# Attention head statistics in four partition groups

## The reference, cut to what matters

```python
h = rmsnorm(x, p['mix_norm'])
z = h @ p['w_in']                       # q 12x128 | k 12x128 | v 12x128 | u | gates
q = z[..., :ATT_WIDTH].reshape(B, L, N_ATT_HEADS, HEAD_DIM)
k = z[..., ATT_WIDTH:2 * ATT_WIDTH].reshape(B, L, N_ATT_HEADS, HEAD_DIM)
q = rope(rmsnorm(q, p['q_norm']), pos)
k = rope(rmsnorm(k, p['k_norm']), pos)

def rmsnorm(x, gain):                   # here over the 128 channels of one head
    y = x * rsqrt(mean(x * x, axis=-1) + 1e-6)
    return y * gain
```

## Time and profile before

| | |
|---|---|
| three timed runs | 2300.42, 2302.45, 2301.75 us; median 2301.75 |
| the profiled execution | 2301.55 us, of which the span of the trace is 2299.8 us |
| granted TensorE clock, mean | 0.998 of full speed |
| busy in the span | PE 2272.1 us (99%), DVE 1404.6 (61%), ACT 995.0 (43%), POOL 535.9 (23%) |
| iterations x = 1 to 12 | about 880 to 1033 us of the span, clock 1.00 |

### The profile page before, as it was taken

The page is one execution under the profiler, slowest core; times in us unless marked ns, Lnnn a source line. Parts: engine busy times, 40 slices in busy tenths (PEclk is TensorE's granted clock), DMA queues, the critical chain, the costliest instruction groups (busy, mean ns, idle before and its releaser), DMA issues.

```text
span 2299.8 us, 47445 instructions
## 1 busy us (share of the span) xinstructions
PE 2272.1 (99%) x18546; PEld 2255.7 (98%) x18546; DVE 1404.6 (61%) x1414; ACT 995.0 (43%) x1219; POOL 535.9 (23%) x565
## 2 busy tenths in 40 slices
PE   7999999999999999999999999999999999999999
PEld 7999999999999999999999999999999999999998
DVE  6566457775455667886657777655554455544555
ACT  5644333333344543444445555444433344333442
POOL 3795026650000204664405540110000000000000
PEclk9999999999999999999999999999999999999999
DMA  7888777777777688758848865568787777657864
GB/s 209 265 246 284 227 242 248 256 260 246 236 238 224 202 262 260 229 180 284 300 145 307 283 197 186 174 202 270 239 243 224 241 246 250 219 184 222 246 199 139
DMA packets 435222, 535.65 MB, mean 233 GB/s; under 512 B 27744, under 2 KB 415832, under 8 KB 431272
## 3 DMA queue, kind: packets, MB, share of 16 engines
q1 hardware_dynamic: 420224, 511.58, 70.7%
q0 software_dynamic: 3216, 11.75, 1.5%
q10 hardware_dynamic: 11680, 10.91, 1.4%
HBM read 510.95 MB, written 109.10 MB: 270 GB/s over the span
## 4 chain that ended last, share of the span: by engine, by line
PE 87%; DVE 5%; POOL 3%; issue 2%; DMA 1%; ACT 1%; SPq 0%; ACTq 0%; DVEq 0%
PE pa L1313 28%; PE pa L1314 27%; PE pa L1315 27%; DVE w_lo L927 2%; POOL c_exp L1781 1%; DVE head_sd L1088 1%; POOL pre L1777 1%; DMA raw<-in_ffn_w_up 1%; PE pb L1411 1%; PE pb L1586 1%; ACT w_hi L586 1%; PE pb L1571 1%; DVE up_v L1092 0%; DMA raw<-in_ffn_w_gate 0%; DVE xg_lo L934 0%
## 5 line engine op out<-in xcount | busy, mean ns | idle before, releaser
L927 DVE TENSOR_TENSOR w_lo<-raw,w_hi 128x1024 fp32r<-128x1024 f32 x736 | 937.0, 1287 | 643.9 <-ACT w_hi L586 639.3
L1313 PE MATMUL pa<-xg_hi,w_hi 128*128 128x264 f32 x3968 | 1137.5, 287 | 9.1 <-DVE w_lo L927 5.8
L1314 PE MATMUL pa<-xg_lo,w_hi 128*128 128x264 f32 x3968 | 1129.1, 285 | 0.0
L1315 PE MATMUL pa<-xg_hi,w_lo 128*128 128x264 f32 x3968 | 1127.9, 284 | 0.0
L586 ACT ACTIVATE w_hi<-raw 128x1024 fp32r<-128x1024 f32 x736 | 767.3, 1055 | 734.4 <-PE pa L1315 708.4
L1313 PEld LDWEIGHTS pa<-xg_hi,w_hi 128*128 128x128 f32 x3968 | 748.7, 189 | 13.8 <-DVE w_lo L927 6.3
L1314 PEld LDWEIGHTS pa<-xg_lo,w_hi 128*128 128x128 f32 x3968 | 747.3, 188 | 0.6
L1315 PEld LDWEIGHTS pa<-xg_hi,w_lo 128*128 128x128 f32 x3968 | 747.5, 188 | 0.0
L1314 PE MATMUL pa<-act_lo,w_hi 128*128 128x264 f32 x1632 | 463.8, 284 | 0.0
L1313 PE MATMUL pa<-act_hi,w_hi 128*128 128x264 f32 x1632 | 463.5, 284 | 0.0
L1315 PE MATMUL pa<-act_hi,w_lo 128*128 128x264 f32 x1632 | 463.1, 284 | 0.0
(11 more groups left out here) (315 smaller groups left out, 1653.6 us busy)
## 6 DMA issues: line engine op xcount, KB each, us to landing
raw<-in_ffn_w_gate SPq DMA_DIRECT2D x172, 512.0 KB, 4.7
raw<-in_ffn_w_up SPq DMA_DIRECT2D x172, 512.0 KB, 5.5
out_kv_s<-in_cache_kv_w SPq DMA_DIRECT2D x165, 512.0 KB
raw<-in_ffn_w_down SPq DMA_DIRECT2D x160, 512.0 KB, 4.5
raw<-in_w_in SPq DMA_DIRECT2D x152, 512.0 KB, 5.1
raw<-in_w_out SPq DMA_DIRECT2D x32, 512.0 KB, 4.4
tab<-ssm_tab SPq DMA_DIRECT2D x8, 1664.0 KB, 8.9
raw<-in_w_ssm_branch SPq DMA_DIRECT2D x16, 512.0 KB, 3.9
```

Of the source, the lines that this page charges most:

```text
L927: dve.tensor_tensor(w_lo[:, slot], raw[:, slot], w_hi[:, slot].bitcast(f32), ALU.subtract).then_inc(lo_ready, 1)
L1313: pe.matmul(out, wh, hi, start=first, stop=False)
L1314: pe.matmul(out, wh, lo, start=False, stop=False)
L1315: return pe.matmul(out, wl, hi, start=False, stop=last)
```

## The change

The 264 tokens of a head are cut into four quarters of 66. `head_stats` now makes eight products: quarter q of head u goes to partitions 32q to 32q+31 of `pb` bank 0, columns 66u to 66u+65, with only 32 columns of `head_w` as weights. Both heads then lie in 132 columns on all 128 partitions, so one root (128x132) and one reciprocal (128x132) do what a root of 128x528 and two reciprocals of 128x264 did. `head_sd` shrinks to 132 columns.

The inverse roots then lie only on their quarter's partitions. `inverse_to_all`, new and placed on PE after slab 2, makes four products with one row each: row 32q of `head_sd` (132 columns) times a row of ones, to `pb` bank q on all 128 partitions. `head` (both heads now at j = 3) multiplies `gate_v` and gain with the inverse roots out of PSUM, four runs of 66 columns. Since all four banks of `pb` are used for this, the turning of k and v pairs moves: pairs 6 to 9 to j = 1 of iterations 9 to 12, pairs 10, 11 and 12 to j = 1, 2 and 3 of iteration 13, pairs 13 to 17 to j = 2 of iterations 14 to 18. `head_stats` waits for `t1_ready` instead of `head_sd_ready`, the root for `inv_wide`.

```diff
     ssq = tile("ssq", [P, 2, T], f32, RQ)
     qb0 = tile("qb0", [P, NSLOT * HD], f32, RT + 32 * T)
     qb = [qb0, qb1]
-    head_sd = tile("head_sd", [P, 2, T], f32, RQ)
+    head_sd = tile("head_sd", [P, 2 * T // 4], f32, RQ)
+    QT = T // 4
 
     QKV = 4 * (2 * NH * T + 2 * NH * HD)
     RM = region(QKV)
...
 
         return PH["q"].group0 + x
 
-    def turned_pairs(x):
-
-        return [x - 2] * (6 <= x - 2 < 12) + [x - 1] * (12 <= x - 1 < 18)
+    def turned_pairs(x, j):
+
+        if x == 13:
+            return [9 + j] if j else []
+        return [x - 3] * (j == 1 and 6 <= x - 3 < 10) + [x - 1] * (j == 2 and 13 <= x - 1 < 18)
 
     K_STORED, QK_STORED, ROWS_STORED = 48, 80, 144
     SAMPLES = NG * NS * NSLOT
...
                 if j == 1 and 1 <= x <= NH:
                     act.wait_ge(stat_done, x)
                     if x >= 2:
-                        act.wait_ge(t1_ready, 2 * (x - 1))
-                    act.activation(head_sd[:], pb[:, 0:2, 0:T], ACT.Sqrt, bias=eps_t).then_inc(head_sd_ready, 1)
+                        act.wait_ge(inv_wide, x - 1)
+                    act.activation(head_sd[:], pb[:, 0, 0:2 * QT], ACT.Sqrt, bias=eps_t).then_inc(head_sd_ready, 1)
                 if j == 3 and x < NH:
                     act.wait_ge(evacuated, pair_group(x) + 1)
                     if x:
...
 
             def head_rows(x, j):
 
-                if j == 3:
-                    for e in turned_pairs(x):
+                if j:
+                    for e in turned_pairs(x, j):
                         c0 = 256 * (e % 2)
                         act.wait_ge(heads_t, e - 5)
                         rows = pb[:, 2, :].rearrange("p (a b) -> p a b", a=2)
...
                 dve.wait_ge(u_ready, i + 1)
                 dve.sem_inc(evacuated, 1)
 
-            def head(x, u):
+            def head_inverse(x):
 
                 dve.wait_ge(head_sd_ready, x + 1)
-                dve.reciprocal(head_sd[:, u], head_sd[:, u]).then_inc(head_inv, 1)
-                dve.wait_ge(head_inv, 2 * x + u + 1)
-                if x and u == 0:
+                dve.reciprocal(head_sd[:], head_sd[:]).then_inc(head_inv, 1)
+
+            def head(x):
+
+                dve.wait_ge(inv_wide, x + 1)
+                if x:
                     dve.wait_ge(qk_ready, 2 * x)
-                dve.scalar_tensor_tensor(up_v[:, u], gate_v[:, u], vec[:, V_HEAD + 2 * x + u:V_HEAD + 2 * x + u + 1],
-                                         head_sd[:, u], ALU.mult, ALU.mult).then_inc(t1_ready, 1)
+                for u in range(2):
+                    dve.scalar_tensor_tensor(up_v[:, u].rearrange("p (q c) -> p q c", q=4), gate_v[:, u].rearrange("p (q c) -> p q c", q=4),
+                                             vec[:, V_HEAD + 2 * x + u:V_HEAD + 2 * x + u + 1], pb[:, :, QT * u:QT * u + QT],
+                                             ALU.mult, ALU.mult).then_inc(t1_ready, 1)
 
             def attention(i, j):
                 h = i // 2
...
                         if name == "gates_a":
                             attention(i, j)
                             decode(i, j)
-                        if j >= 2 and 1 <= x <= NH:
-                            head(x - 1, j - 2)
+                        if j == 2 and 1 <= x <= NH:
+                            head_inverse(x - 1)
+                        if j == 3 and 1 <= x <= NH:
+                            head(x - 1)
                         n = ph.slab0 + 4 * i + j - PH["v"].slab0 - UNIT_USE
                         if 0 <= n < len(UNITS):
                             g, b = UNITS[n]
...
             def head_stats(x):
 
                 pe.wait_ge(head_sq, x)
-                pe.wait_ge(*((sd_ready, 2) if x == 1 else (head_sd_ready, x - 1)))
+                pe.wait_ge(*((sd_ready, 2) if x == 1 else (t1_ready, 2 * (x - 1))))
                 for u in range(2):
-                    ins = pe.matmul(pb[:, u, 0:T], head_w[:], sq_v[:, u, :], start=True, stop=True)
+                    for q in range(4):
+                        ins = pe.matmul(pb[32 * q:32 * q + 32, 0, QT * u:QT * u + QT], head_w[:, 0:32], sq_v[:, u, QT * q:QT * q + QT],
+                                        start=True, stop=True)
                 ins.then_inc(stat_done, 1)
 
+            def inverse_to_all(x):
+
+                pe.wait_ge(head_inv, x)
+                if x >= 9:
+                    pe.wait_ge(rows_ready, x - 8)
+                for q in range(4):
+                    ins = pe.matmul(pb[:, q, 0:2 * QT], ones[32 * q:32 * q + 1, :], head_sd[32 * q:32 * q + 1, :], start=True, stop=True)
+                ins.then_inc(inv_wide, 1)
+
             def heads_to_rows(x, j):
 
-                if j == 3:
-                    for e in turned_pairs(x):
+                if j:
+                    for e in turned_pairs(x, j):
+                        if x == NH + 1:
+                            pe.wait_ge(t1_ready, 2 * NH)
                         if e < 12:
                             pe.wait_ge(qk_ready, 2 * e + 2)
                         else:
...
                             mean_square(1)
                         if j == 1 and 1 <= x <= NH:
                             head_stats(x)
+                        if j == 2 and 1 <= x <= NH:
+                            inverse_to_all(x)
                         heads_to_rows(x, j)
                         if name == "gates_a":
                             attention(i, j)
```

More of the change, by code:

```diff
@@ L321, in build_layer @@
     u_ready, u4_zero, u4_loaded, spilled, const_loaded = sems("u_ready u4_zero u4_loaded spilled const_loaded")
-    head_sq, stat_done, head_sd_ready, head_inv, t1_ready, rot_ready, cos_ready, qk_ready = sems(
-        "head_sq stat_done head_sd_ready head_inv t1_ready rot_ready cos_ready qk_ready")
+    head_sq, stat_done, head_sd_ready, head_inv, inv_wide, t1_ready, rot_ready, cos_ready, qk_ready = sems(
+        "head_sq stat_done head_sd_ready head_inv inv_wide t1_ready rot_ready cos_ready qk_ready")
     heads_t, rows_ready, rows_stored, v_new_ready, samples_t, samples_ready, qk_new_ready = sems(
```

## The result

The changed kernel is slower, by much less than forecast: a median of 2308.93 us (2308.22 to 2310.86, 10 runs) against 2302.57 (2300.42 to 2303.99, 10 runs) beside it, a ratio of 1.0031 [1.0023, 1.004] over all runs (the two medians alone give 1.0028). That is 0.3%, small but clear of the noise. Forecast were 2321.8 us, and the range began at 2310. The profiled execution took 2310.86.

A forecast was written before the change was run, and what follows sets the result against it. PE, busy 2272.1 of 2299.8 us, bounds the kernel. Statistics and copy back 12 x (0.21 + 1.1) = 15.7, plus 6.8 of waits, minus 2.3 for late squares: +20.2 on 2301.55, so 2321.8 us, range 2310 to 2332.

The forecast's parts named there:

- statistics on PE: Eight 66-column products, sixteen records, in each of twelve iterations: +0.07 to +0.36 us a pair, taken as +0.21.
- products that copy back: New one-row products on PE after slab 2, eight records of 132 columns: 0.64, 1.16 or 1.58 us, taken as +1.1 a pair.
- wait for the reciprocal: PE held before the copy-back products: 0.45 us in eight iterations, 0.70 in two, 0.91 in two, 6.8 in all.
- late squares: Head iterations where PE's statistics wait for squares, with the chain over DVE: 2.3 us lost, all that the change can regain.
- transposes moved: Transposes of k and v pairs at new places: same number, no cost change of their own outside the wait.
- Neither row has 66 columns, so I take the middle: Statistics block on PE: between lower end +0.07 and upper end +0.36 us a pair, +0.21 chosen.
- Middle of the ends: Copy-back block on PE: price between 0.64 and 1.58 us, +1.1 a pair chosen.
- rival A: Groups overlap on PE, spacings fall to 0.036 us: statistics +0.07, copy back 0.64, +13 in all, 2314.6 us; chance 0.25.
- change-over: Leaving and entering the full array around a block of small products on PE: 0.39 us a block besides its inner spacings.
- rival C: Not slower: copy-back block's price after slab 2 goes towards nothing, at 0.1 us a pair 2300.5 us; chance 0.07.
- Rival D: Longer wait before the copy-back products, ACT or DVE late: 1.2 us a pair, +7.6 on the forecast, 2329.4 us; chance 0.08.
- time lost after 1045 us: Sign of being wrong: loss in the v or gates phases of the old span, where none was expected.

The follow-up runs named there:

- e3: Changed kernel without the four one-row products that copy back, so q and k are normalised with wrong numbers: 2293.58 us, 0.9963 of the kernel before.
- e1: Changed kernel with DVE making the reciprocal ahead of its split of the same slab, not behind it: 2301.42 us, 0.9996 of the kernel before.
- e6: Kernel before the change, with ACT's squares of a pair moved behind the next iteration's first split: 2299.22 us, 0.9991.
- e4: Changed kernel with all eight statistics products on one 32-column group, the first 32 partitions: 2316.68 us, 1.0065 of the kernel before.
- e5: Changed kernel with the four one-row copy-back products all taken from partition 0, one row group: 2318.84 us, 1.0077 of the kernel before.
- e8: e7 with pair 11 transposed at j = 2 of iteration 13 instead of j = 3: 2291.81 us, 0.9956 of the kernel before.
- e7: e6 with squares and `head_w` also written rounded (fp32r), so each statistics product is one record: 2291.61 us, 0.9955 of the kernel before.
- the repeat: The changed kernel profiled and measured again with no edit, beside the kernel before: 2309.26 us, ratio 1.003.

## Why the prediction was wrong

The sign was right and so was most of the account; two sizes in it were not, and one term stood at nothing that was something. Term by term, in us over the head part:

| term | forecast | measured | shown by |
|---|---|---|---|
| statistics on PE, 12 times | +0.21 each, +2.5 | -0.30 each, -3.6 | e3 (12.53 to 12.23), rows of after |
| products that copy back, 12 times | +1.1 each, +13.2 | +0.64 each, +7.6 | e1 less e3 |
| wait for the reciprocal | +6.8 | +7.7 | after less e1 |
| late squares | -2.3 | -2.3 | e6 |
| transposes moved | 0 | -1.3 | what is left of e3 |
| sum | +20.2 | +8.1 | |

*The step that failed* is "Neither row has 66 columns, so I take the middle", and "Middle of the ends" for the copies. The statistics came out 6.1 us cheaper than forecast and the copies 5.6, of the 12.1 us by which the sum was too high (the wait was 0.9 short, and the transposes gave 1.3 more). The bounds were made of rows in which one group works at a time, and e4 and e5 show that for one group they were good: 1.23 and 1.29 us, the forecast's 1.22 and a little over its 1.16. But the change uses four, and then the records start in fours. In the trace of after, the sixteen of the statistics start at 881.951, .958, .965, .971, then from 882.033 the same, from 882.091 and from 882.148: 6 to 7 ns apart within a four, 0.04 to 0.06 us between fours. The eight copies: four at 885.974 to .994, four at 886.191 to .211. So what queues is the records of one group, and four groups queue at once. On one group (e4, e5) records of 66 columns stand 0.056 to 0.062 apart and of 132 columns 0.112. One spacing, the first, is longer in each block, with four groups or with one: 0.082 for the statistics and 0.217 for the copies, and the latter just as much where nothing is waited for (e1). Why is open. The forecast's upper end for the copies rested on such a one: the 0.17 of L1552 is the first and only spacing of its block. The argument against rival A, that the order is group by group with both records of a product together, did not hold; whether the list on the chip has another order or PE passes one group's second record by can't be seen, since the records don't name their group.

The rule that was weighed said this. The Trainium skill's "TensorE: Matmul & The Clock Gate", Part 3, has products on different groups start about 4 ns apart; here it was 6 to 7 ns. It was given a quarter of the chance: no row showed two groups in use, and the order seemed to speak against it. The sign that the forecast had named for A, sixteen statistics records within 0.5 us, came (0.22). Rival A, which stood for the rule, was the nearest on the sum (2314.6). That it has the copies at 0.64, right to the hundredth, is luck: seven spacings of 0.036 happen to fill what one of 0.197 and six of 7 ns or less fill, 0.24. And it was still too dear on the statistics: it took over a floor of 0.036 a record from L1544, which is again the spacing in one group, and got +0.07 where -0.30 was measured. Had the rule been followed into the terms (four groups at once), the statistics' sixteen records would have had three spacings of 0.055 between four rounds, and their block would have come to 0.39 + 0.17 + 0.02 = 0.58, for 0.57. For the copies it would have been one spacing of 0.11: 0.39 + 0.11 + 0.02 = 0.52, too cheap by the long first spacing.

*The change-over* of 0.39 a block, from L1411, held to 0.04: it is 0.35 in the statistics' block (0.57 less 0.22 of spacings) and 0.40 in that of the copies (0.64 less 0.24), and the same with one group in e4 and e5. It is about 60% of what either block costs. This is why rival C, a block price near zero, was wrong, and why these thin blocks stayed dear even though their groups overlap.

*The wait* was right in its mechanism, place, count and shape over the iterations, and a little short: 0.45, 0.70 and 0.91 us were forecast, 0.54, 0.74 and 0.94 measured. By the earlier trace rows against the rows above: the root starts 0.07 after the last record and not 0.03, takes 0.37 at 132 columns and not 0.26, and the split follows at 0.34 and not at 0.19. From there the forecast's 1.09, 1.14 and 0.97 are 1.08, 1.14 and 0.97. Against that, the 0.1 added for weights that can't be loaded ahead of the wait did not show: the copies' records start at the same distances, and cost the same up to the second slab product, behind the wait (after) and with none (e1). Rival D (1.2 us a pair) was wrong. What the forecast did not see is that only the order makes this wait, reciprocal behind split, and that the split can take the delay: in e1 it is 1 us later and PE is busy through the whole stretch of 12.86.

*Late squares*: right to 0.02.

*The transposes*: "The number of transposes stays" was right and "cost what they did" wrong, by 1.3 us. This is the term that was put at nothing. About 0.3 of it, read from the iterations and not tried apart: right after the statistics the two share one change-over, and a pair of iterations 11 and 12 adds 0.38 us (12.61 - 12.23 in e3) and not the 0.46 that it adds in e6 (12.99 - 12.53). About 1.0: in iteration 13 each pair now has its own slab, and the second need not wait for ACT's copy of the first. That iteration takes 12.99 (11.67 and three times 0.44) for 13.51 although it transposes one pair more. The wait of 0.78 us stood in the trace of before, and e8, which changes nothing else against e7, gains 0.96 there.

*Nothing outside* the head part: what the rest of the span lost or won against before lies, in every trace, in the first 80 slabs or between slabs 402 and 432, to 0.1, and has either sign. The forecast named time lost after 1045 us as a sign of being wrong, and the first trace has +1.2 there; but it lies in the stretch of half clock, and the repeat has nothing there.

## What to carry to other kernels

When a change uses a resource in a way that the trace before doesn't show, here several groups of the array at once, bounds from rows with one in use are bounds for another case: take the mechanism (what queues behind what) and not the middle. Small products cost their change-over here, 0.35 to 0.40 us a block between full-array products, more than their columns; so the first question is whether they can be kept in the neighbours' form, which was worth more (-9.7 us for e6 and e7 together) than the whole scheme of groups (-7.3 at best, without the way back). And where an engine off the critical path makes something that the critical one waits for, look at what stands ahead of it in its own list: moving one reciprocal ahead of one split gave back 7.7 of 8.1 us. Last, a mean over instructions that run beside different neighbours can hide two kinds, as that of DVE's product did.

## What was not expected of the hardware

- Full-float32 products on four column groups: 16 records of 66 columns in 0.22 us, 6 to 7 ns apart in fours; on one group 0.89 us. One-row products on four row groups: 8 records of 132 columns in 0.24 us; on one group 0.89.
- In both blocks the four groups saved the same 0.65 us, though one has twice the records of half the columns. It is the columns that count: twelve spacings of 66 columns fewer in one block, six of 132 in the other, 792 both times.
- The first slab product behind either block is followed by the second only 0.23 us later (882.32 to 882.55), not 0.12. This 0.11 of the change-over is paid after the block, by a product that looks ordinary.
- DVE's product with the inverse roots, both tensors in SBUF, took 0.49 us with POOL idle and 0.80 to 0.83 with POOL's rotary beside it. With the inverse roots in PSUM it took 0.48 either way. So the place of that factor hardly changed the product's own speed, but what POOL's work beside it costs; no run varied this alone. The difference makes 5.1 of the 9 us by which DVE lost more than the forecast's 31.
- A stretch of half clock (0.51) fell once into the head part, in e5, and cost 1.5 us: 15 slab products at 0.22 us, which is the lower of TensorE's two levels (1.2 GHz, for 2.4 before and after it).
